# Unread products of constants on TensorE in five waits for norms, and low-part products chunk by chunk

## The chip, the core and the metric

The kernel runs on one core of a Trainium2 chip. Its time is the device time of one execution in microseconds (us); shown are the median of three executions and one execution taken with the hardware profiler. PE is TensorE, PEld its weight loads, DVE VectorE, ACT ScalarE, POOL GpSimd, SP the engine that issues the weight transfers. "L420" is line 420 of the kernel.

## What is computed

Two transformer stacks of two layers each, on 256 tokens of width 1024, all in float32. The parts that matter here are the norms and the projections behind them:

```python
def rms_norm(x, g):
    xf = x.astype(jnp.float32)
    y = xf * lax.rsqrt(jnp.mean(xf * xf, axis=-1, keepdims=True) + EPS)
    return y.astype(x.dtype) * g
...
# first_block, layer l (twice)
        x = x + gt1_x * (jnp.concatenate([oa, ob, oc], axis=-1) @ w_out[l])
        hx2 = modulate(rms_norm(x, g_norm2[l]), sh2_x, sc2_x)
        x = x + gt2_x * conv_ffn(hx2, w_up[l], conv_w[l], conv_b[l], w_down[l])
...
# second_block, layer l (twice)
        h = rms_norm_2(x, norm_mix_pre[l])
        proj = h @ w_in[l]
        ...
        x = x + rms_norm_2(merged @ w_out[l], norm_mix_post[l])
        h2 = rms_norm_2(x, norm_ffn_pre[l])
        gu = h2 @ w_ffn_in[l]
        f_g, f_u = jnp.split(gu, 2, axis=-1)
        f = (jax.nn.silu(f_g) * f_u) @ w_ffn_out[l]
        x = x + rms_norm_2(f, norm_ffn_post[l])
```

The first block also carries a second stream (`ctx`) of 256 tokens through its first layer.

## The kernel before

The activations stand transposed: eight chunks of 128 features by 256 tokens. A float32 operand is cut into a high part (type fp32r, written by ACT) and a low part (the rest, written by DVE or POOL), and a projection is three products of that type for each chunk: high by high, low weight by high, high weight by low. A weight tile is 1024 columns wide, which gives 128 output features in 24 products (L406, L407, L408 in `products`). SP brings the tiles in, ACT cuts off the high part (L1005) and DVE the low part (L1637); four cut tiles have room, and the room of a tile comes free when its last product is done (`lin`).

Each engine has its own program in a fixed order, written out as the Python code runs, and engines meet at semaphores. Results go to four PSUM banks in turn (`PS`); a fifth tile waits until the first one's bank has been read.

Where an activation has only just been normed, the first two weight tiles go through `two_tiles` instead. PE first takes the products with the high parts: for the first tile, chunk by chunk as ACT delivers (L420 and L421, each pair waits for `x_hi` of its chunk), then for the second tile, sixteen products with nothing to wait for. Then follow the products with the low parts (L428): all eight of the first tile, then all eight of the second. It is called 13 times. In the feed-forward of the second block `between` puts the eight sums of the `fpre` norm between the high and the low products.

A norm needs a sum over all 1024 features. ACT squares the chunks, PE adds them up by a product with a matrix of ones in plain float32 (`SquareSum`, L481), ACT takes the root (L1067), DVE the reciprocal (L1673), and then the normed chunks are made. A plain float32 product stands in the trace as two records, so the eight sums of a norm are 16 records. Three norms are summed in another form (`in_groups`): `x0`, `fpost` and `pre` of the second layer. There four squares are summed at a time, each on 32 columns of the array (L469), ACT copies the four partial sums out (L1064), and a product with the constant `four` adds them (L487) before ACT takes the root.

Five places are spoken of below, in order of time. At each, PE has finished the sums of a norm and waits for root, reciprocal and the first normed chunk:

- **A**: first block, second layer, before the feed-forward.
- **B**: between the first and the second block.
- **C**: second block, first layer, between `w_out` (norms `post` and `fpre`) and the feed-forward.
- **D**: second block, between its layers: norm `fpost`, then norm `pre`.
- **E**: as C, in the second layer.

Of the kernel before, what the change touches and what calls it, by code (L numbers as in the profile page):

```python
# [153 lines left out]
def build(nc, w_d, par_d, con_d, big_d, x_d, pos_d, out_d, widths):  # L154
    PAR, npar, CON, ncon = offsets()
    ctx = ExitStack()
    with ctx:
# [40 lines left out]
        ident, ones, eps = con("ident"), con("ones"), con("eps")  # L198
# [95 lines left out]
        def in_groups(tag):  # L294

            return tag == "x0" or tag[0] in ("fpost", "pre")
# [95 lines left out]
        def tensor(q):  # L392
# [18 lines left out]
            def two_tiles(src, at, between=None):  # L411
                us = [feed.next() for _ in range(2)]
                bk = [PS.take() for _ in us]
                for b, i in zip(bk, us):
                    w = weights(i, 8)
                    q.wait_ge(*cut(i))
                    wait(b.free)
                    for c in range(8):
                        q.wait_ge(*at[c][0])
                        e.matmul(b.ap[:, 0:256], w.hi[:, c], src[c].hi, start=c == 0, stop=False)  # L420
                        e.matmul(b.ap[:, 0:256], w.lo[:, c], src[c].hi, start=False, stop=False)  # L421
                if between is not None:
                    between()
                for b, i in zip(bk, us):
                    w = weights(i, 8)
                    for c in range(8):
                        q.wait_ge(*at[c][1])
                        last = e.matmul(b.ap[:, 0:256], w.hi[:, c], src[c].lo, start=False, stop=c == 7)  # L428
                    last.then_inc(*lin.mark(i))
                for i in us:  # L430
                    feed.release(i)
                return list(zip(bk, us))
# [11 lines left out]
            class SquareSum:  # L444
# [38 lines left out]
                def rstd(self, out):  # L483
# [4 lines left out]
                    self.bank.free = [roots(self.tag)]  # L488

# [174 lines left out]
            def feed_forward(tag, at, passed, early=None, between=None):  # L664
                bk, tiles = [], {}
                got = two_tiles(H8, at, between)
# [39 lines left out]
            for l in range(DEPTH):  # L706
# [87 lines left out]
                else:  # L794
                    ss_x.rstd(k.rst[0])
                    feed_forward(("ffn", l, 0), parts_of(("n2", l, 0)), convd)
# [5 lines left out]
                    ss.rstd(k.rst[0])  # L802

            for l in range(DEPTH):
                at = parts2_of(("pre", l))
                lows = []
                for n in range(2):
                    sq = SquareSum(("low", l, n), 2)
                    got = two_tiles(H8, at) if n == 0 else [tile(H8), tile(H8)]
# [169 lines left out]
                ss.rstd(k.rst[0])  # L979
                ss = SquareSum(("fpre", l), 8, k.sq2[0])  # L980
# [9 lines left out]
                if l + 1 < DEPTH:  # L990
                    ss = SquareSum(("pre", l + 1), 8)
# [4 lines left out]
                    ss.rstd(k.rst[0])  # L996

# [1908 lines left out]
```

## Time and profile before

| | us |
|---|---|
| median of three executions | 2258.08 |
| lowest, highest | 2256.72, 2259.97 |
| profiled execution, its own time | 2255.04 |
| span of its trace | 2253.2 |

The clock that the chip granted to PE is 0.972 of full speed in the mean: it is either full (2.4 GHz) or half (1.2 GHz). Busy time of PE is no measure of its work, since products overlap: a product of 256 columns lasts 0.28 us in the trace, but at full clock the next starts 0.117 us later. So the text counts from start to start. In a timeline row, the first number is the start and the second the length; "xN" says how many instructions are merged; the last bracket tells how long the engine was idle and which engine's instruction released it.

### The profile page before, as it was taken

To read this page: it belongs to the slowest core of one execution; us is meant where nothing else is said; L and a number is where in the kernel's file an instruction comes from. 1 tells how busy PE (TensorE), PEld (TensorE's weight loads), DVE (VectorE), ACT (ScalarE), POOL (GpSimd) and SP (SyncE) were. 2 spreads that over 40 slices of the span, in tenths; PEclk is the share of its full clock that TensorE was granted. 3 is DMA by queue.
4 is the path that set the end of the run, shared out by engine and by line. 5 is a ranking of instruction groups with operands and counts; after the bars stand their busy time and mean duration, and the time that the engine had idled before them with its cause. 6 is when DMAs were issued, how large, how long until landed. Compare 5 with 4: busy or idle time off the path is not lost.

```text
span 2253.2 us, 43766 instructions
## 1 busy us (share of the span) xinstructions
PE 2110.4 (94%) x18160; PEld 1970.9 (87%) x18160; DVE 1514.5 (67%) x2244; ACT 1150.2 (51%) x1919; POOL 561.5 (25%) x668
## 2 busy tenths in 40 slices
PE   6999989999999999899999989989997989999997
PEld 5986679999999886689988889989996889998997
DVE  3657766777777666668776769755556677865554
ACT  4535545555655643555556555554444655554443
POOL 0012321332333002213321144104330134212331
PEclk9999999999999998999999999999998999999999
DMA  8546544555555454345544335535552434453552
GB/s 345 178 143 230 206 169 147 191 188 171 168 196 184 140 163 159 129 143 192 191 159 155 131 118 183 179 121 197 188 188 105 158 114 150 144 196 133 190 191 85
DMA packets 103205, 378.37 MB, mean 168 GB/s; under 512 B 11456, under 2 KB 11744, under 8 KB 101984
## 3 DMA queue, kind: packets, MB, share of 16 engines
q1 hardware_dynamic: 101520, 367.31, 47.6%
q10 hardware_dynamic: 1488, 8.27, 1.0%
q8 instruction: 144, 2.36, 0.4%
q14 instruction: 53, 0.43, 0.1%
HBM read 374.49 MB, written 1.05 MB: 167 GB/s over the span
## 4 chain that ended last, share of the span: by engine, by line
PE 33%; issue 13%; POOL 5%; DVE 3%; ACT 3%; POOLq 0%; DVEq 0%; ACTq 0%
PE ps L406 10%; PE ps L408 10%; PE ps L407 10%; POOL R L2596 2%; POOL R L2638 1%; DVE WL L1637 1%; PE ps L481 1%; POOL R L2441 1%; PE ps L420 1%; POOL X L2399 1%; PE ps L421 1%; ACT WH L1005 1%; PE ps L428 1%; DVE RST L1673 1%; DVE TMP L1647 0%
## 5 line engine op out<-in xcount | busy, mean ns | idle before, releaser
L406 PE MATMUL ps<-X,WH 128*128 128x256 f32 x4384 | 1242.6, 283 | 15.3 <-DVE WL L1637 7.9
L407 PE MATMUL ps<-X,WH 128*128 128x256 f32 x4384 | 1228.4, 280 | 0.0
L408 PE MATMUL ps<-X,WL 128*128 128x256 f32 x4384 | 1227.4, 280 | 0.0
L1637 DVE TENSOR_TENSOR WL<-RAW,WH 128x1024 fp32r<-128x1024 f32 (+2 forms) x608 | 773.6, 1290 | 452.9 <-ACT WH L1005 451.1
L406 PEld LDWEIGHTS ps<-X,WH 128*128 128x128 f32 x4384 | 827.0, 189 | 30.0 <-DVE WL L1637 11.7
L407 PEld LDWEIGHTS ps<-X,WH 128*128 128x128 f32 x4384 | 826.9, 189 | 1.7
L408 PEld LDWEIGHTS ps<-X,WL 128*128 128x128 f32 x4384 | 826.9, 189 | 0.0
L1005 ACT ACTIVATE WH<-RAW 128x1024 fp32r<-128x1024 f32 (+2 forms) x608 | 623.8, 1045 | 263.6 <-PE ps L408 261.5
L2441 POOL TENSOR_SCALAR R<-CONS,SM 128x128 f32<-128x128 f32 x128 | 83.8, 666 | 319.6 <-DVE SM L1832 308.9
L2535 POOL TENSOR_TENSOR TMP<-TMP 128x256 f32<-128x256 f32 x66 | 48.9, 741 | 446.6 <-ACT TMP L1354 443.1
L1155 ACT ACTIVATE PB<-ps,SM 128x512 f32<-128x512 f32 (+1 forms) x152 | 87.6, 583 | 140.9 <-DVE SM L1822 140.5
L1647 DVE SCALAR_TENSOR_TENSOR TMP<-ps,PARS,TMP 128x255 f32<-128x255 f32 x264 | 124.2, 480 | 11.4 <-ACT TMP L1350 2.7
L1647 DVE SCALAR_TENSOR_TENSOR R<-R,PARS 128x256 f32<-128x256 f32 x180 | 109.7, 662 | 0.0
L2540 POOL TENSOR_TENSOR X<-TMP,X 128x256 fp32r<-128x256 f32 x66 | 103.6, 1570 | 5.3
L1350 ACT ACTIVATE TMP<-ps,PARS 128x256 f32<-128x256 f32 x132 | 71.5, 555 | 58.5 <-PE ps L408 52.1
L1822 DVE TENSOR_REDUCE SM<-ps 128x1 f32<-128x512 f32 (+2 forms) x136 | 77.1, 606 | 27.6 <-PE ps L609 26.9
L420 PE MATMUL ps<-X,WH 128*128 128x256 f32 x208 | 66.4, 344 | 30.5 <-ACT X L1609 10.6
L1354 ACT ACTIVATE TMP<-TMP 128x256 f32<-128x256 f32 x66 | 27.6, 418 | 116.1 <-DVE TMP L1647 116.1
L643 PEld LDWEIGHTS ps<-PTB,R 128*64 128x64 f32 x768 | 43.1, 139 | 49.5 <-issue 23.4
L2656 POOL TENSOR_TENSOR TMP<-TMP,RST 128x256 f32<-128x256 f32 x44 | 32.6, 741 | 210.4 <-ACT TMP L1617 210.3
L643 PE MATMUL ps<-PTB,R 128*64 128x128 f32 x768 | 59.6, 286 | 24.7 <-ACT PTB L1170 18.2
L420 PEld LDWEIGHTS ps<-X,WH 128*128 128x128 f32 x208 | 49.1, 236 | 36.9 <-issue 22.4
(194 smaller groups left out, 2204.0 us busy)
## 6 DMA issues: line engine op xcount, KB each, us to landing
RAW<-w_dram SPq DMA_DIRECT2D x674, 512.0 KB, 3.7
RAW<-w_dram SPq DMA_DIRECT2D x16, 480.0 KB, 3.2
BIG<-big_dram ACTq DMA_DIRECT2D x4, 1024.0 KB, 5.2
RAW<-w_dram SPq DMA_DIRECT2D x8, 320.0 KB, 2.7
RAW<-w_dram SPq DMA_DIRECT2D x6, 384.0 KB, 2.9
XT<-x_dram ACTq DMA_DIRECT2D x2, 1024.0 KB, 7.5
CONS<-con_dram ACTq DMA_DIRECT2D x1, 1169.0 KB, 9.7
out_dram<-XT SPq DMA_DIRECT2D x1, 1024.0 KB, 3.9
```

What stands on the lines that cost most here:

```text
L406: e.matmul(out, a.hi, b.hi, start=start and i == 0, stop=False, skip_group_check=open_bank)
L407: e.matmul(out, a.hi, b.lo, start=False, stop=False, skip_group_check=open_bank)
L408: last = e.matmul(out, a.lo, b.hi, start=False, stop=stop and i == n - 1, skip_group_check=open_bank)
L420: e.matmul(b.ap[:, 0:256], w.hi[:, c], src[c].hi, start=c == 0, stop=False)
L643: e.matmul(ob[0].ap[64 * s:64 * s + 64, c:c + 128], u["subs"][s]["v"][j], b[:, 128 * j:128 * j + 128], start=j == 0, stop=j == nk - 1)
L1005: e.activation(weights(i).hi, raw(i), ACT.Copy).then_inc(*w_hi.mark(i))
L1155: e.activation(ap, bank.ap[:, x * u["nk"]:x * u["nk"] + u["nk"]], ACT.Exp, bias=sm.ap[:, col:col + 1], accum_out=sm.ap[:, 4 + col:5 + col] ...
L1637: e.tensor_tensor(weights(i).lo, raw(i), weights(i).hi.bitcast(F32), ALU.subtract).then_inc(*w_lo.mark(i))
L1647: return e.scalar_tensor_tensor(out=out, in0=a, scalar=s, in1=b, op0=o0, op1=o1)
L1822: e.tensor_reduce(sm.ap[:, col:col + w], bank.ap[:, 0:w * nk].rearrange("p (x n) -> p x n", x=w), AX, ALU.max, negate=True).then_inc(*maxe ...
L2441: e.tensor_scalar(d.ap, ident, sm.ap[:, 8 + s:9 + s], None, ALU.mult).then_inc(*inverted.mark(tag, i, s))
L2540: e.tensor_tensor(a.ap.lo, bg.ap, a.ap.hi.bitcast(F32), ALU.subtract).then_inc(*gate_lo.mark(tag, j))
```

## The change

It adds a helper `keep_up(n, cols)` to the PE program. It issues n products of the matrix of ones with the constant `cosA`, in plain float32, into the next free PSUM bank. Nobody reads them, and no mark is set.

- `keep_up` stands behind the sums of a norm at A (6 products), B (6), C and E (11 each), and twice at D (9 behind `fpost`, 6 behind `pre`).
- In four of the 13 calls of `two_tiles` (`fill`: behind B, C, D and E) one product of 256 columns follows each chunk's high-part pair of the first tile (7 times), and one of 64 columns each chunk's low-part pair (7 times). At A the call has no such filling.
- In all 13 calls the low-part products go chunk by chunk: chunk 0 for both tiles, then chunk 1 for both, and so on.
- `fpost` and `pre` are no longer summed in groups; the form with eight products and no copy is used, for `fpost` of both layers and for `pre` of the second.

```diff
         def in_groups(tag):
-            return tag == "x0" or tag[0] in ("fpost", "pre")
+            return tag == "x0"
...
-            def two_tiles(src, at, between=None):
+            def two_tiles(src, at, between=None, fill=False):
...
                         e.matmul(b.ap[:, 0:256], w.lo[:, c], src[c].hi, start=False, stop=False)
+                        if fill and b is bk[0] and c < 7:
+                            keep_up(1)
                 if between is not None:
                     between()
-                for b, i in zip(bk, us):
-                    w = weights(i, 8)
-                    for c in range(8):
+                for c in range(8):
+                    for b, i in zip(bk, us):
                         q.wait_ge(*at[c][1])
-                        last = e.matmul(b.ap[:, 0:256], w.hi[:, c], src[c].lo, start=False, stop=c == 7)
-                    last.then_inc(*lin.mark(i))
+                        last = e.matmul(b.ap[:, 0:256], weights(i, 8).hi[:, c], src[c].lo, start=False, stop=c == 7)
+                        if c == 7:
+                            last.then_inc(*lin.mark(i))
+                    if fill and c < 7:
+                        keep_up(1, 64)
...
+            def keep_up(n, cols=256):
+
+                bank = PS.bufs[PS.n % len(PS.bufs)]
+                q.wait_ge(s_con2, 16)
+                wait(bank.free)
+                for _ in range(n):
+                    e.matmul(bank.ap[:, 0:cols], ones, con("cosA")[:, 0:cols], start=True, stop=True)
...
-                got = two_tiles(H8, at, between)
+                got = two_tiles(H8, at, between, fill=between is not None)
...
                     ss_x.rstd(k.rst[0])
+                    keep_up(6)
                     feed_forward(("ffn", l, 0), parts_of(("n2", l, 0)), convd)
...
                     ss.rstd(k.rst[0])
+                    keep_up(6)
...
-                    got = two_tiles(H8, at) if n == 0 else [tile(H8), tile(H8)]
+                    got = two_tiles(H8, at, fill=True) if n == 0 else [tile(H8), tile(H8)]
...
                 ss.rstd(k.rst[0])
+                keep_up(11)
                 ss = SquareSum(("fpre", l), 8, k.sq2[0])
...
                 if l + 1 < DEPTH:
+                    keep_up(9)
                     ss = SquareSum(("pre", l + 1), 8)
...
                     ss.rstd(k.rst[0])
+                    keep_up(6)
```

PE's program at D, before: the two grouped sums, then the first high-part pairs. `scaled`, `squares` and `parted` are marks of DVE and ACT, `ps` is PSUM, R and PB hold squares, CONS the constants.

```order
L469 MATMUL ps<-R,CONS 32x256 [waits scaled,squares]
L469 MATMUL ps<-R,CONS 32x256 x3
L469 MATMUL ps<-R,CONS 32x256 [waits squares]
L469 MATMUL ps<-R,CONS 32x256 x3
L487 MATMUL ps<-RST,CONS 128x256 [waits parted]
L469 MATMUL ps<-PB,CONS 32x256 [waits squares,scaled]
L469 MATMUL ps<-PB,CONS 32x256 x3
L469 MATMUL ps<-PB,CONS 32x256 [waits squares]
L469 MATMUL ps<-PB,CONS 32x256 x3
L487 MATMUL ps<-RST,CONS 128x256 [waits parted]
L420 MATMUL ps<-X,WH 128x256 [waits x_hi,w_lo]
L421 MATMUL ps<-X,WL 128x256
```

The same place of PE after the change, where L485 is the former L481 and L500 the product in `keep_up`:

```order
L485 MATMUL ps<-R,CONS 128x256 [waits squares]
L485 MATMUL ps<-R,CONS 128x256
L500 MATMUL ps<-CONS 128x256 x9
L485 MATMUL ps<-PB,CONS 128x256 [waits scaled,squares]
L485 MATMUL ps<-PB,CONS 128x256 [waits squares] x7
L500 MATMUL ps<-CONS 128x256 x6
L420 MATMUL ps<-X,WH 128x256 [waits x_hi,w_lo]
L421 MATMUL ps<-X,WL 128x256
L500 MATMUL ps<-CONS 128x256
L420 MATMUL ps<-X,WH 128x256 [waits x_hi]
L421 MATMUL ps<-X,WL 128x256
```

The product with `four` and its wait are gone, eight full products per norm stand in place of two groups of four, and every high-part pair has an unread product between it and the next.

PE's program at the end of the same call of `two_tiles` in B, before: the low-part products, the first tile's with their waits and then the second tile's.

```order
L428 MATMUL ps<-X,WH 128x256 [waits x_lo] x2
L428 MATMUL ps<-X,WH 128x256 [waits y_lo]
L428 MATMUL ps<-X,WH 128x256 [waits x_lo] x2
L428 MATMUL ps<-X,WH 128x256 [waits y_lo]
L428 MATMUL ps<-X,WH 128x256 [waits x_lo] x2
L428 MATMUL ps<-X,WH 128x256 x8
L406 MATMUL ps<-X,WH 128x256 [waits convd,w_lo]
```

And after (L429 is the former L428):

```order
L429 MATMUL ps<-X,WH 128x256 [waits x_lo]
L429 MATMUL ps<-X,WH 128x256
L500 MATMUL ps<-CONS 128x64
L429 MATMUL ps<-X,WH 128x256 [waits x_lo]
L429 MATMUL ps<-X,WH 128x256
L500 MATMUL ps<-CONS 128x64
```

The first tile's last product now stands next to last instead of eighth, and seven narrow products stand in between.

## Rows read from the trace of the kernel before

The columns of a window row are its start and end, its length, each engine's busy time with its instructions (x), PE's granted clock, the busy share of the DMA engines, and GB/s. A timeline row has start, length, engine, line and operation; the bracket holds the idle time before it and what ended it. Windows of one engine hold PE alone; windows of all engines hold PE, PEld, DVE, ACT and POOL.

**Rows 1.** The page: full products and their weight loads, busy and mean ns.

```profile
L406 PE MATMUL ps<-X,WH 128*128 128x256 f32 x4384 | 1242.6, 283 | 15.3 <-DVE WL L1637 7.9
...
L406 PEld LDWEIGHTS ps<-X,WH 128*128 128x128 f32 x4384 | 827.0, 189 | 30.0 <-DVE WL L1637 11.7
```

**Rows 2.** PE: feed-forward behind C by window; next long wait behind D.

```profile
1520.84:1700.04 179.20, 179.20 (x1538) 1.00 0.56 191
...
1754.53 0.36 PE L406 MATMUL ps<-X,WH 128*96 128x256 f32 x1 [1.80 <-ACT R L1424]
```

**Rows 3.** PE by windows at A to E, last sum to third tile.

```profile
977.31:989.14 11.83, 8.25 (x50) 0.71 0.15 51
1175.08:1187.05 11.97, 8.56 (x49) 0.71 0.05 17
1501.94:1520.84 18.90, 13.47 (x66) 0.73 0.07 26
1703.99:1726.79 22.80, 11.48 (x68) 0.63 0.03 9
2040.28:2059.65 19.37, 13.95 (x66) 0.74 0.06 23
```

**Rows 4.** Timeline of PE: first high-part product at C.

```profile
1507.02 0.55 PE L420 MATMUL ps<-X,WH 128*128 128x256 f32 x1 [4.91 <-ACT X L1609]
```

**Rows 5.** Timeline of PE in B: two products at half clock.

```profile
1183.75 0.41 PE L420 MATMUL ps<-X,WH 128*128 128x256 f32 x1
1183.96 0.41 PE L421 MATMUL ps<-X,WL 128*128 128x256 f32 x1
```

**Rows 6.** Timeline: eight float32 sums in C; weights of an 8-column product.

```profile
1515.52 3.62 PE L481 MATMUL ps<-R,CONS 128*128 128x256 f32 x16
...
192.41 0.30 PEld L497 LDWEIGHTS ps<-CONS,R 128*128 128x128 f32 x2 [1.21 <-DVE R L1702]
```

**Rows 7.** All engines by window, high-part products of an unfilled call.

```profile
1473.96:1479.48 5.52, 4.61 (x34) 3.99 (x33) 3.06 (x6) 4.51 (x9) 1.60 (x2) 1.00 0.35 123
```

**Rows 8.** All engines by window, the same pause in either layer.

```profile
1407.70:1414.70 7.00, 3.89 (x27) 3.54 (x26) 7.00 (x12) 0.84 (x2) 0.53 (x2) 1.00 0.24 74
1943.30:1950.30 7.00, 3.92 (x11) 3.05 (x10) 7.00 (x12) 0.84 (x2) 0.52 (x2) 0.66 0.24 78
```

**Rows 9.** Timeline of ACT: eight high parts at A, five at B.

```profile
980.41 3.30 ACT L1087 ACTIVATE X<-TMP,SM 128x256 fp32r<-128x256 f32 x8 [2.42 <-DVE TMP L1647]
...
1178.09 2.00 ACT L1392 ACTIVATE X<-TMP 128x256 fp32r<-128x256 f32 x5 [2.34 <-DVE TMP L1647]
```

**Rows 10.** Timeline of ACT: the last two high parts in C.

```profile
1510.62 0.90 ACT L1609 ACTIVATE X<-XT,PARS 128x256 fp32r<-128x256 f32 x2
```

**Rows 11.** Timeline of PE: first grouped sum of D, whole sum at B.

```profile
1701.61 1.19 PE L469 MATMUL ps<-R,CONS 128*32 128x256 f32 x16 [1.42 <-ACT R L1053]
...
1171.55 3.69 PE L481 MATMUL ps<-R,CONS 128*128 128x256 f32 x16 [1.33 <-DVE XT L1647]
```

**Rows 12.** Timeline of ACT at D: root, last squares, second root.

```profile
1704.09 0.47 ACT L1067 ACTIVATE RST<-ps,CONS 128x256 f32<-128x256 f32 x1 [0.79 <-PE ps L487]
...
1711.63 0.72 ACT L1044 ACTIVATE PB<-XT 128x256 f32<-128x256 f32 x2 [0.18 <-PE ps L469]
...
1715.38 0.47 ACT L1067 ACTIVATE RST<-ps,CONS 128x256 f32<-128x256 f32 x1 [1.31 <-PE ps L487]
```

**Rows 13.** Timeline, last norm: PE's first sums, ACT's root.

```profile
2238.94 0.64 PE L469 MATMUL ps<-R,CONS 128*32 128x256 f32 x8
...
2241.71 0.47 ACT L1067 ACTIVATE RST<-ps,CONS 128x256 f32<-128x256 f32 x1 [0.79 <-PE ps L487]
```

**Rows 14.** Timeline in `w_out`: ACT's first square, PE's first sum.

```profile
1480.62 0.38 ACT L1044 ACTIVATE PB<-ps 128x256 f32<-128x256 f32 x1 [0.92 <-PE ps L428]
...
1481.35 0.60 PE L481 MATMUL ps<-PB,CONS 128*128 128x256 f32 x2
```

**Rows 15.** Timeline of PE: sums behind the first call of `two_tiles`.

```profile
43.94 3.72 PE L481 MATMUL ps<-R,CONS 128*128 128x256 f32 x16 [1.26 <-ACT R L1053]
```

## The prediction

> **What bounds the kernel now.** I read the page first, then PE by windows, then the timelines at the places that the diff touches. The table ahead has the span, 2253.2 us; the execution's own time is 2255.04, and the median, 2258.08, lies 3.0 above. Over long stretches PE is the bound: behind C it runs 64 weight tiles, 1536 products, in 179.2 us without a pause at full clock [rows 2]. That is 0.117 us from start to start and 2.8 a tile, though each lasts 0.283 [rows 1], and whatever delays PE there delays the end. The pauses stand where a norm must be known. At the five places of the change PE waits between the last sum and the first high-part product, 4.9 us at C [rows 4] and about 3.5 at A and B, and the granted clock in the windows from the last sum to the third weight tile is 0.63 to 0.74 of full [rows 3]: it falls to half in the pause and comes back in or behind the products. At half clock they start 0.21 us apart [rows 5]. The chain in the pause (root, reciprocal, scaling) is ACT's and DVE's and doesn't care for PE's clock. So what a full clock can give back is only in the products behind it, and it must be weighed against what the unread products cost once real work is ready.
>
> **Prices.** Eight float32 sums are 16 records in 3.62 us [rows 6], of which the last one's length beyond its step is some 0.17 (0.283 less 0.117, as for a real product): 0.215 a record, 0.43 a product of 256 columns at full clock. A filled pair then takes 2 x 0.117 + 0.43 = 0.665 us, an unfilled one 0.235. For 64 columns no row exists. By columns alone it would be a quarter, 0.11 us. But each of its two records also loads 128 columns of weights, and the two loads of an 8-column product take 0.30 us together, 0.11 more than the 0.189 of one [rows 1, 6]; in the stream of real products a record never costs under 0.117 [rows 2]. I take 2 x 0.117 = 0.23, nearest to that row, and keep 0.11 and, above, 0.43 for the range. Seven of them cost 1.6 us a call.
>
> The Trainium skill (FP8 and Floating Point Precision, TensorE Precision Notes) says that true FP32 takes four passes through the array. For 64 columns this would be 4 x 64 / 2.4 GHz = 0.11 us, and the 28 narrow products would cost 3.5 us less than in my sum. TensorE: Matmul & The Clock Gate, LDWEIGHTS (loading the stationary operand), has a weight load depend on its columns alone, 128 / 1.2 = 107 ns each, whatever the product's width; the row's 0.11 agrees with it.
>
> **Does the clock hold?** At A, B, D the six unread products cover 2.6 of some 3.5 us, at C and E eleven cover 4.7 of 4.9. The rest, about 1 us, is far below any pause behind which the clock fell here: the same 3.4 us pause was followed by full clock in one layer and by 0.66 in the other [rows 8]. Nor do paused high-part pairs bring it down: an unfilled call took 5.52 us at 1.00 [rows 7]. I take full clock at all five.
>
> **A** (no filling). Eight high parts come 0.4 us apart, the last at 983.71 [rows 9]. The last pair of the first tile then ends near 984.1, 16 products of the second tile at 985.98, 16 low-part ones at 987.85. The low parts follow the high ones 2.6 us behind, and going by chunks lets PE start on them without a wait. Before: 989.14 [rows 3]. **-1.3.**
>
> **B** (filled). The high parts come 0.4 apart [rows 9], but a filled pair takes 0.665: now PE, not ACT, sets the pace. From 1178.6, plus 0.1 for a start out of idleness, 7 x 0.665 + 0.235 gives 1183.55; 16 products, 1185.4; 16 low-part products and seven narrow ones, 1.87 + 1.6, 1188.9. Before: 1187.05. **+1.9.**
>
> **C and E** (filled). The high parts come slower here, the last at 1511.52 [rows 10], so the filling costs only 0.3: first tile done at 1512.1, second 1513.95, eight sums 1517.4, low parts 1520.9. Before: 1520.84, and that with half clock in much of it. **0.** E paid 19.37 for what C did in 18.90 [rows 3]; in the profiled execution it would gain 0.4. That is chance, so I count E as C.
>
> **D.** The first grouped sum starts at 1701.61 [rows 11] and its root at 1704.09 [rows 12]. A whole sum needs 3.7 us from its start to the root [rows 11], 1705.3: +1.2, on the chain. For `pre` the four last squares end at 1712.35 and the root follows only at 1715.38, 3.0 later: four products, a copy and the product with `four`, at half clock [rows 12]. Eight products keep up with the squares, and only one is left behind the last: 0.9. That gives 2.1 back, net -0.9. The filling is B's: from 1717.8 to 1728.1. Before: 1726.79. **+1.3.**
>
> **Last norm.** Sums start at 2238.94, root at 2241.71 [rows 13]. Whole: 16 x 0.215 + 0.2 = 3.65 from the start, 2242.6. Nothing stands behind it but the chain to the output. **+0.9.**
>
> **Low parts by chunks, elsewhere.** The first tile ends seven products (0.8 us) later, the second at the same time. This costs where somebody waits for the first one. Behind `w_out`, PE's first sum waits for ACT's square of it: 1480.62 to 1481.00, the sum at 1481.35 without a wait [rows 14]. Now the square starts at 1481.4, the sum at 1481.9: +0.65, twice. **+1.3.** In the first call the sums wait for ACT too [rows 15], behind its square and copy of both tiles, which now come together: **+0.4.** In the other calls ACT's work on the first tile has slack, since bank and weights are due 5.6 us later: 0. PE waited for no low part, so the new order gains nothing. DMAs and SP's queue are untouched.
>
> **Sum:** -1.3 + 1.9 + 0 + 0 + 1.3 + 0.9 + 1.3 + 0.4 = +4.5 us (4.1 against the profiled execution, with E's 0.4). The terms before rounding (-1.29, 1.86, 0.05, 0, 1.35, 0.88, 1.30, 0.45) give 4.6. On the median: 2258.1 + 4.6 = 2262.7.
>
> **Rivals.**
> (1) *The delay behind B and D is taken up.* PE's next long wait behind D, 1.8 us, ends with ACT's L1424 [rows 2]. If ACT's and DVE's chain before it doesn't start from PE's third tile, B's and D's 1.9 + 1.3 vanish: 2259.5. Against it: that chain starts with PE's sums of `low`, which stand behind those tiles.
> (2) *Narrow products cost their columns only*, 0.11: 28 x 0.12 = 3.4 less, 2259.3.
> (3) *Faster.* The profiled execution was 3.0 below the median. If that is half clock that others pay at these five places, it is gone now, and the sum starts from 2255.0: 2259.2; with (2) as well, 2255.8, and with (1) too, 2252.6. It decides from all three together on. For it: the length of a half-clock stretch is chance [rows 3, 8]. Against it: the rest of the kernel has such stretches too.
> (4) *The clock falls all the same.* Then filling is dear: at half clock a filled pair takes 1.3 us. Seven more expensive pairs and 16 products at 0.21, +6 us at B and at D each: up to 2274.
>
> The Trainium skill (TensorE: Matmul & The Clock Gate, Why this matters for your kernels) asks for no idle gap over some 3 us, which speaks against the filling: the 1 us left by the six products would be harmless by it. No run here shows B without filling; by the working of A it would end 3 us earlier.
>
> **How the numbers follow.** The measurement tells a change of about 0.2%, 4.5 us, from none: slower begins at 2262.6, faster below 2253.6. Forecast as worked out, give or take 2 us: 0.60, of which 0.40 above 2262.6, since the half-clock stretches of other executions can be shorter than those profiled. (1) 0.10 and (2) 0.10, both no change. (3) 0.10, of which 0.06 faster. (4) and a narrow product at 0.43 (5.6 more): 0.10, slower. Together: slower 0.40 + 0.10 = 0.50, faster 0.06, within 0.2% the other 0.44. The likeliest case is spread over the edge; its own range is 2260 to 2265.5. The range from (2) with part of (3) to the dear end: 2256.5 to 2268.5.
>
> **What would show it.** A profile of the changed kernel should have: a clock of 1.00 at A to E; starts 0.215 apart in the unread products of 256 columns and 0.117 in those of 64; at B and D no idleness between high-part pairs, and 10.3 us from the first of them to the third tile; at A 6.9; sums of the last norm in 3.7 us; PE's first sum behind `w_out` 0.6 us later than the low parts' end. The prediction is wrong if the narrow records start closer, if the wait behind D shrinks by what the tiles lost, or if the clock is below 1 in any of the five.

## The result, and the profile after

The changed kernel is slower by 0.41%: median 2266.72 us of eight executions (2261.11 to 2270.97) against 2256.43 of before (2252.84 to 2260.34), ratio 1.0041, 95% interval 1.0029 to 1.0053, or 9.2 us (6.5 to 12.0); the two medians as they stand are 10.3 us apart. A second set of executions of both kernels gave 1.0035 (1.0023 to 1.0048). The forecast was 2262.7, 4.6 us more than before. The direction held, and 2266.7 lies in the range of 2256.5 to 2268.5, but above the likeliest case of 2260 to 2265.5; the forecast change was about half of the measured one.

The profiled execution took 2261.11 us, the shortest of the eight, with a span of 2259.3 us and a mean clock of 0.984 (before: 2253.2 us and 0.972). So the clock rose as the change meant it to, and the kernel still lost time. The lines are moved: L429 is the former L428, L485 the former L481, L500 the unread product; L1061, L1070, L1084, L1409, L1441 and L1654 are the former L1044, L1053, L1067, L1392, L1424 and L1637.

PE by windows in the changed kernel, from the last sum to the third tile, places A to E (the answers to [rows 3]; columns as there):

```profile
980.44:990.97 10.53, 9.54 (x61) 1.00 0.12 44
1177.43:1191.30 13.87, 13.05 (x90) 1.00 0.09 30
1504.67:1523.67 19.00, 18.83 (x115) 1.00 0.07 25
1707.98:1730.98 23.00, 21.19 (x124) 1.00 0.05 18
2045.97:2064.96 18.99, 18.83 (x116) 1.00 0.07 25
```

The clock is 1.00 in all five, where it was 0.63 to 0.74. A is 1.3 us shorter. B is 1.9 longer although its clock rose from 0.71. C is 0.1 longer and E 0.4 shorter. D by this window is 0.2 longer, but it begins behind `fpost`'s sums; with these it is 1.35 longer, as shown below.

Timeline of PE at B: the filled pairs, and the narrow products between low-part products.

```profile
1181.20 0.28 PE L421 MATMUL ps<-X,WL 128*128 128x256 f32 x1
1181.32 0.59 PE L500 MATMUL ps<-CONS 128*128 128x256 f32 x2
...
1181.87 0.28 PE L421 MATMUL ps<-X,WL 128*128 128x256 f32 x1
...
1188.10 0.33 PE L500 MATMUL ps<-CONS 128*128 128x64 f32 x2
1188.24 0.48 PE L429 MATMUL ps<-X,WH 128*128 128x256 f32 x2
1188.56 0.33 PE L500 MATMUL ps<-CONS 128*128 128x64 f32 x2
```

Read the starts. From one filled pair to the next (1181.20 to 1181.87) it is 0.67 us, forecast 0.665. From one pair of low-part products with its narrow product to the next (1188.10 to 1188.56) it is 0.46, of which the pair is 0.23: the narrow product costs 0.23, as taken. One sign did not come as forecast: the two records of a narrow product start 0.055 us apart, not 0.117. Its price holds all the same, since the real products beside it are held up for the rest.

Timeline of PE at D, from `fpost`'s first sum to the first high-part product:

```profile
1704.45 3.69 PE L485 MATMUL ps<-R,CONS 128*128 128x256 f32 x16 [1.42 <-ACT R L1070]
1707.98 4.05 PE L500 MATMUL ps<-CONS 128*128 128x256 f32 x18
1712.88 4.40 PE L485 MATMUL ps<-PB,CONS 128*128 128x256 f32 x16 [0.85 <-ACT PB L1061]
1717.11 2.75 PE L500 MATMUL ps<-CONS 128*128 128x256 f32 x12
1720.68 0.36 PE L420 MATMUL ps<-X,WH 128*128 128x256 f32 x1 [0.82 <-ACT X L1409]
```

and of ACT there, the two roots and the last squares between them:

```profile
1708.18 0.47 ACT L1084 ACTIVATE RST<-ps,CONS 128x256 f32<-128x256 f32 x1 [3.32 <-PE ps L485]
...
1714.81 1.34 ACT L1061 ACTIVATE PB<-XT 128x256 f32<-128x256 f32 x4 [0.48 <-DVE XT L2349]
1717.31 0.47 ACT L1084 ACTIVATE RST<-ps,CONS 128x256 f32<-128x256 f32 x1 [1.16 <-PE ps L485]
```

The root of `fpost` comes 3.73 us behind the first sum (2.48 in [rows 11, 12]), that of `pre` 1.16 behind the last square (3.03). First sum to third tile is 1730.98 - 1704.45 = 26.53; before it was 1726.79 - 1701.61 = 25.18. PE's next long wait behind D is still there at its length, 27.75 us behind the third tile (27.74 before [rows 2]), so this delay isn't taken up there:

```profile
1758.73 0.36 PE L406 MATMUL ps<-X,WH 128*96 128x256 f32 x1 [1.81 <-ACT R L1441]
```

Timeline in `w_out` (answers to [rows 14]) and in the last norm (to [rows 13]):

```profile
1483.54 0.38 ACT L1061 ACTIVATE PB<-ps 128x256 f32<-128x256 f32 x1 [1.74 <-PE ps L429]
1483.98 0.70 PE L485 MATMUL ps<-PB,CONS 128*128 128x256 f32 x2 [0.36 <-ACT PB L1061]
...
2244.16 3.61 PE L485 MATMUL ps<-R,CONS 128*128 128x256 f32 x16
2247.81 0.47 ACT L1084 ACTIVATE RST<-ps,CONS 128x256 f32<-128x256 f32 x1 [2.86 <-PE ps L485]
```

PE's first sum now waits 0.36 us for ACT's square where it did not wait, and the call with its sum takes 8.26 us instead of 7.63. The last norm's root comes 3.65 us behind the first sum, where it came 2.77 behind.

So every term of the sum that stood for something is there at its size, and yet the median moved by twice the sum. The spans of the two profiled executions differ by 6.1 us, of which the terms are 4.1 (with E's 0.4, as the forecast had it for this pair). Stretches between the places that were to stay the same differ by 2.8 us one way and 2.1 the other, with 2.0 left over. Where the rest comes from is the question of the experiments.

### The profile page after: what moved, and what is told of

Read it like the earlier page. It is cut to its first block, busy times and chain, and to the rows that moved or that the text cites. A ratio compares the mean times of both kernels' runs of the same rounds, so it can differ in the third digit from the quotient of the medians.

```text
span 2259.3 us, 44160 instructions
## 1 busy us (share of the span) xinstructions
PE 2138.5 (95%) x18364; PEld 1998.7 (88%) x18364; DVE 1514.9 (67%) x2244; ACT 1148.6 (51%) x1916; POOL 561.3 (25%) x668
## 4 chain that ended last, share of the span: by engine, by line
PE 33%; issue 13%; POOL 5%; DVE 4%; ACT 2%; POOLq 0%; DVEq 0%; ACTq 0%
PE ps L406 10%; PE ps L407 9%; PE ps L408 9%; POOL R L2613 2%; POOL R L2655 1%; DVE WL L1654 1%; PE ps L485 1%; POOL R L2458 1%; PE ps L500 1%; POOL X L2416 1%; ACT WH L1022 1%; PE ps L420 1%; PE ps L429 1%; DVE RST L1690 1%; DVE TMP L1664 1%
## 5 line engine op out<-in xcount | busy, mean ns | idle before, releaser
L406 PE MATMUL ps<-X,WH 128*128 128x256 f32 x4384 | 1242.0, 283 | 17.8 <-DVE WL L1654 8.8
L407 PE MATMUL ps<-X,WH 128*128 128x256 f32 x4384 | 1226.7, 280 | 0.0
L1654 DVE TENSOR_TENSOR WL<-RAW,WH 128x1024 fp32r<-128x1024 f32 (+2 forms) x608 | 773.7, 1290 | 459.2 <-ACT WH L1022 457.5
L406 PEld LDWEIGHTS ps<-X,WH 128*128 128x128 f32 x4384 | 825.4, 188 | 31.4 <-DVE WL L1654 12.7
L407 PEld LDWEIGHTS ps<-X,WH 128*128 128x128 f32 x4384 | 825.6, 188 | 1.6
L1664 DVE SCALAR_TENSOR_TENSOR TMP<-ps,PARS,TMP 128x255 f32<-128x255 f32 x264 | 124.1, 480 | 11.8 <-ACT TMP L1367 3.1
L2557 POOL TENSOR_TENSOR X<-TMP,X 128x256 fp32r<-128x256 f32 x66 | 103.5, 1569 | 5.3
L2655 POOL TENSOR_TENSOR R<-R,TMP 128x256 f32<-128x256 f32 x48 | 38.7, 821 | 154.4 <-DVE TMP L2295 154.4
L2681 POOL TENSOR_TENSOR X<-TMP,X 128x256 fp32r<-128x256 f32 x44 | 73.9, 1680 | 3.5
```

The source lines that it names most:

```text
L406: e.matmul(out, a.hi, b.hi, start=start and i == 0, stop=False, skip_group_check=open_bank)
L407: e.matmul(out, a.hi, b.lo, start=False, stop=False, skip_group_check=open_bank)
L1654: e.tensor_tensor(weights(i).lo, raw(i), weights(i).hi.bitcast(F32), ALU.subtract).then_inc(*w_lo.mark(i))
L1664: return e.scalar_tensor_tensor(out=out, in0=a, scalar=s, in1=b, op0=o0, op1=o1)
L2557: e.tensor_tensor(a.ap.lo, bg.ap, a.ap.hi.bitcast(F32), ALU.subtract).then_inc(*gate_lo.mark(tag, j))
L2681: e.tensor_tensor(a.ap.lo, b.ap, a.ap.hi.bitcast(F32), ALU.subtract).then_inc(*gate_lo.mark(("glu", l), j))
```

## The experiments

Twelve runs were made: nine new kernels, and before, the changed kernel and one of the nine a second time. Ratios are to the executions of before in the same set, with 95% intervals; 0.001 is 2.3 us. "Call" is the time from the first high-part product of `two_tiles` to the third tile.

### How much of it is before's own spread

> The kernel before, unchanged, to see how much its executions differ and with what clock. The changed kernel lost 9.2 us in the medians (6.5 to 12.0), but the terms of the forecast, which its profile bears out place by place, give 4.6. Theory: the profiled execution of before (2255.0 us, clock 0.972) paid more at the five places than its executions do on average, since the clock falls and comes back at other moments; then the executions here spread over some 8 us, with clocks from 0.970 to 0.980, and in a second profile the five windows from the last sum to the third tile together are shorter than the 84.9 us of the first by 1 to 5 us. Rival: the five windows are as long as in the first profile within 1 us, and the difference arises in stretches that the change doesn't touch.

> The changed kernel, unchanged, for a second set of executions. Its profile bore out every term of the forecast within 0.1 us, which sum to 4.6 us, but its median lay 9.2 us (6.5 to 12.0) above before. Executions of before alone spread from 2249 to 2261 us. Theory: the surplus is chance of that spread in 8 executions; here the median is 2261 to 2265, ratio to before 1.003 (1.0015 to 1.004). Rival: the surplus is real and lies in stretches that the change doesn't touch: 2266 to 2268, ratio 1.004 or above, and the stretches from the first narrow call of two_tiles to the next two (266.46 and 185.10 us in the first profile, 263.69 and 182.60 in that of before) are again 2 us longer each.

Measured: before against itself 1.0002 (0.999 to 1.0015). Twelve executions took 2252.91 to 2261.55 us, with clocks of 0.969 to 0.977. In its profile the five windows are together 0.7 us shorter than in the first, so the rival held. That what separates executions of before, some 9 us, lies elsewhere is likely but not shown, since only a few executions have a profile. Four profiles with before's form at the five places (these two and two from below) gave calls of 7.9 to 8.2 us at A, 8.2 to 8.5 at B, 13.5 to 14.4 at C and E. The half clock there was not dearer in the profiled execution than it commonly is.

The changed kernel again: 1.0035 (1.0023 to 1.0048), median 2263.31, as the theory had it. The calls at A to E are the same to 0.02 us as in its first profile. Of the stretches named in the rival, the one up to the narrow call (the third call of `two_tiles`, at some 370 us) had 264.9 us, so that surplus doesn't come every time; the one behind it had 183.7 where before had 182.6 in both profiles. That one goes with the order, as the next three kernels show.

### The filling, and the order of the low parts

`no_fill`, then `order_back` on top of it, then `order_alone`, which is before with the new order and nothing else:

```diff
-                got = two_tiles(H8, at, between, fill=between is not None)
+                got = two_tiles(H8, at, between, fill=False)
...
-                    got = two_tiles(H8, at, fill=True) if n == 0 else [tile(H8), tile(H8)]
+                    got = two_tiles(H8, at) if n == 0 else [tile(H8), tile(H8)]
```

```diff
-                for c in range(8):
-                    for b, i in zip(bk, us):
+                for b, i in zip(bk, us):
+                    w = weights(i, 8)
+                    for c in range(8):
...
```

> The changed kernel without the unread products inside two_tiles (28 of 256 and 28 of 64 columns gone); those in the waits stay, and the order of low parts and the whole sums too. Theory: the clock is held by the products in the waits alone, so B and D take A's 6.8 us from first high-part product to third tile where they took 10.3, -3.5 each; C and E lose 7 x 0.23 for the narrow ones and 0.3 for the wide ones, -1.9 each. Together -10.8 us against the changed kernel's 2266.7: 2255.9, ratio to before 0.9998 (0.9985 to 1.001). Rival: without the filling the clock falls in the pauses between the pairs, as it did before; B, D stay at 8.0 to 8.4 us, C and E at 13.8 to 14.3, and the kernel takes some 2262, ratio 1.0025.

> As no_fill, and the low parts tile by tile again, as before the change. Theory: going by chunks costs 0.65 us behind each w_out and 0.45 in the first call, and nothing elsewhere, so this is 1.75 us below no_fill; ratio to before 0.999 (0.9978 to 1.0002). In the profile PE's first sum in w_out stands 7.6 us behind the first high-part product again, not 8.26. Rival: with the clock full at A to E the first tile's low parts now come too late (2.6 us behind the high ones), PE waits for them at A, B, D, and what is won at w_out is lost there: same time as no_fill.

> The kernel before with nothing but the low parts chunk by chunk in all 13 calls. Theory: +0.65 behind either w_out and +0.4 in the first call, nothing elsewhere: ratio 1.0008 (0.9995 to 1.002); in the profile the calls behind w_out take 8.26 us where they took 7.63. Rival: the difference of 3.8 us between the two kernels without filling, with and without this order (2258.07 and 2254.29), is the order's own, so that there is another cost, of the first tile of the other calls coming 0.8 us later: ratio 1.0017 or above, with another stretch that is longer by 1 us or more in the profile.

Measured: `no_fill` 0.9998 (0.9988 to 1.0009), `order_back` 0.9989 (0.9976 to 1.0002), `order_alone` 1.0007 (0.9995 to 1.0019).

`no_fill` has the ratio that the theory gave, but its theory, that the waits' products alone hold the clock, is only half true. PE by windows in the calls at B to E, and behind the fall at D:

```profile
1182.95:1190.19 7.24, 6.86 (x48) 1.00 0.02 3
1511.86:1525.49 13.63, 12.11 (x64) 0.87 0.00 0
1722.51:1731.03 8.52, 8.15 (x48) 0.80 0.13 40
2052.76:2065.86 13.10, 11.70 (x65) 0.87 0.01 1
...
1725.03:1728.44 3.41, 3.41 (x17) 0.50 0.00 0
```

B takes 7.24 us instead of 10.29. The filling does have an effect: without it, with the waits still filled, C, D and E fell to half clock for 3.4 us here, at a price of 1.0 to 1.6 us each. At D PE had been idle for 0.82 us ahead of the call and 0.37 in it, no longer at a time. In the four profiles of this form (these waits filled, no filling in the calls) half clock came never at A and B, twice in four at D, and five times in eight at C and E. Against a call at full clock the filling costs 3.1 us at B and at D, and 1.8 at C and at E with its narrow products. Against the mean of the four profiles, half clock included (7.24, 7.87 and 13.0), it costs 3.1 at B, 2.4 at D and 0.9 at C and at E: 7.3 us for which nothing comes back.

`no_fill` and `order_back` differ by 3.8 us in the medians and by 2.0 in the ratios, where 1.75 was expected, and the ratio of `order_alone`, 1.6 us (-1.1 to 4.3), is that of its theory, while its interval just takes in the rival's 1.0017. The times don't decide it. The profile of `order_alone` shows two further delays. First, behind the call at A. ACT in before, then in `order_alone` (third tile at 989.14 and at 995.08):

```profile
989.34 0.56 ACT L1350 ACTIVATE TMP<-ps,PARS 128x256 f32<-128x256 f32 x1 [0.37 <-PE ps L428]
989.92 1.28 ACT L1354 ACT_TABLE_LOAD   x1
...
991.54 2.94 ACT L1005 ACTIVATE WH<-RAW 128x1024 fp32r<-128x1024 f32 x3
```

```profile
995.16 1.02 ACT L1350 ACTIVATE TMP<-ps,PARS 128x256 f32<-128x256 f32 x2 [4.59 <-PE ps L427]
996.20 1.28 ACT L1354 ACT_TABLE_LOAD   x1
...
998.02 2.94 ACT L1005 ACTIVATE WH<-RAW 128x1024 fp32r<-128x1024 f32 x3
```

Both evictions now come at once, so the table load stands 1.12 us behind the third tile's start where it stood 0.78 behind, and the weight splits behind it in ACT's program, L1005, and then DVE's are 0.54 late (998.02 is 2.94 behind the third tile, 991.54 is 2.40). Nobody waits for them at once. PE runs into it 26 us later, in `order_alone`:

```profile
1020.85 0.38 PE L406 MATMUL ps<-X,WH 128*128 128x256 f32 x1 [0.39 <-DVE WL L1637]
```

This wait, some 26 us behind the third tile, stands in all six profiles with the new order and in none of the eight with the old one. From the third tile at A to the first high-part product at B it is 189.5 us in all eight and 190.0 to 190.1 in all six: +0.54.

Second, behind the narrow call at 370 us. PE's next wait there ends with the root of a norm. Timeline of PE in before and in `order_alone`, and the windows of 6 us behind the wait:

```profile
404.40 0.38 PE L406 MATMUL ps<-X,WH 128*128 128x256 f32 x1 [1.70 <-ACT RST L1067]
```

```profile
411.09 0.38 PE L406 MATMUL ps<-X,WH 128*128 128x256 f32 x1 [1.97 <-ACT RST L1067]
```

```profile
404.40:410.40 6.00, 5.50 (x44) 1.00 0.30 104
```

```profile
411.09:417.09 6.00, 6.00 (x38) 0.72 0.36 111
```

The pause is 0.27 us longer and ends 0.54 later behind the call's third tile (31.54 us, before 31.00), and behind it the clock falls. In all six profiles with the new order there is half clock of 3.4 us here and in none of the eight with the old one. The time from the narrow call to the next call of `two_tiles` is 182.6 us in six of these eight (184.0 in the other two) and 183.7 in four of the six (185.1 in the other two): +1.1, of which 0.54 is there when the pause ends and the other 0.6 comes behind it, with the half clock. That the longer pause brought the clock down fits all fourteen profiles, but no run changed the pause alone.

### The sums alone, and in groups again

`sums_alone` against before, and `fpost_grouped` against `order_back`:

```diff
-            return tag == "x0" or tag[0] in ("fpost", "pre")
+            return tag == "x0"
```

```diff
-            return tag == "x0"
+            return tag == "x0" or tag[0] == "fpost"
```

> The kernel before with nothing but whole sums for fpost and pre. Theory: the last norm's root comes 0.9 us later; at D fpost's root 1.2 later. The eight products for pre, which at full clock leave only 0.9 us behind the last square, fall behind the squares here: the clock is half at D, a whole product takes 0.86 us, the squares come in pairs 1.2 us apart, so the root for pre stands 8 x 0.86 = 6.9 us behind the first square at 1708.73 plus what fpost's delay adds: 1716.8, where it was 1715.38. Together +1.4 and +0.9: ratio 1.001 (1.000 to 1.0025). Rival: pre's whole sums give back 2.1 us at half clock too, so D loses nothing net: -0.9 + 0.9 = 0, ratio 1.0000, and the root for pre comes before 1715.5 relative to the same start.

> As order_back, and fpost of both layers summed in groups again; pre of the second layer stays whole. Theory: the last norm's root comes 0.9 us earlier and that of fpost at D 1.2 us earlier, both on the chain, -2.1 against order_back: some 2252.1 by the medians so far, ratio to before 0.998 (0.9968 to 0.9995), faster than both kernels. Rival: at D the gain is lost, since pre's first squares come from DVE, which is busy with the tiles of fpost either way; then -0.9 only.

> fpost_grouped once more, in other executions. Its six executions lay 7.9 us below before, 0.9963. By places and profiles the sum is: A -1.3, B -1.1, C and E -0.9 each, D -0.7 in the call and -1.65 ahead of it (root of fpost no later, pre whole), 0 elsewhere: -6.5 us, 0.9971. Theory: ratio 0.9971 (0.996 to 0.9985), in the profile the calls at A, B, D at 6.8, 7.2 and 7.2 us. Rival: the six were lucky with half clock elsewhere, and by the forecast's own terms (-2.1 against order_back at 0.9989) it is 0.998.

Measured: `sums_alone` 1.0007 (0.9998 to 1.0016), `fpost_grouped` 0.9963 (0.9949 to 0.9977) and again 0.9958 (0.9942 to 0.9973).

ACT at D in `sums_alone`, where PE's first sum starts at 1705.45:

```profile
1709.18 0.47 ACT L1067 ACTIVATE RST<-ps,CONS 128x256 f32<-128x256 f32 x1 [3.33 <-PE ps L481]
...
1719.32 0.47 ACT L1067 ACTIVATE RST<-ps,CONS 128x256 f32<-128x256 f32 x1 [2.17 <-PE ps L481]
```

First sum to the root of `pre` takes 13.87 us; in before it takes 1715.38 - 1701.61 = 13.77. So the theory, that whole sums fall behind the squares at half clock, falls, by the profile: the clock is back before they are through (16 records in 5.41 us against 4.40 at full clock), and `pre` gives back what `fpost` loses. Only the last norm costs: from the third tile at E to the end it takes 194.3 us instead of 193.5. The ratio lies between theory (1.001) and rival (1.0000) and excludes neither.

`fpost_grouped` is faster than both kernels: by 0.37 and 0.42% against before and some 0.8% against the changed one. It keeps the unread products in the waits and whole sums for `pre`, and drops the filling, the new order and `fpost`'s whole sums. Calls at C, D and E in the second profile, PE by windows:

```profile
1503.19:1515.28 12.09, 10.57 (x65) 1.00 0.00 0
1711.04:1719.51 8.47, 8.09 (x48) 0.80 0.12 43
2040.01:2053.65 13.64, 12.12 (x65) 0.87 0.01 1
```

The places give -6.5 us, as its expectation has it; the ratios say -8.3 and -9.5. Both times it came out below the expected range (0.9968 and 0.996). The first expectation put it 2.1 us below `order_back`; it lay 4.9 below in the medians. Two to three us of its gain have no place in the profiles; in the second one D's call even took 8.5 us where 7.2 was expected. How much of the gain is the waits' products and how much `pre`'s whole sums was not run apart.

### Price and purpose of the unread products

`double_fill` and `fill_no_waits` (here B's line; the others likewise) against the changed kernel:

```diff
                         if fill and b is bk[0] and c < 7:
-                            keep_up(1)
+                            keep_up(2)
```

```diff
                     ss.rstd(k.rst[0])
-                    keep_up(6)
+                    keep_up(0)
```

`half_waits` (`keep_up(3)` for 6, 5 for 11, 4 for 9) and `ce_fill` against `fpost_grouped`:

```diff
                     ss.rstd(k.rst[0])
-                    keep_up(6)
+                    keep_up(3)
```

```diff
-                got = two_tiles(H8, at, between, fill=False)
+                got = two_tiles(H8, at, between, fill=tag[0] == "glu")
```

> The changed kernel with two unread products of 256 columns instead of one behind each of the seven high-part pairs (28 more in all). Theory: each costs its two records of 0.215, 0.43 us, on the path: B and D go from 10.29 to 13.3 us, C and E, where a pair has 0.04 of slack, from 13.92 to 16.7. Together +11.6 us against the changed kernel, ratio to before 1.0085 (1.0065 to 1.010). Rival: the stationary operand is the same for both, so the second costs only half, 0.215, as columns alone would have it: +5.6, ratio 1.006 or less, and records half as far apart.

> The changed kernel with the filling in two_tiles, but without the unread products in the waits. Theory (rival 4 of the forecast): the clock falls in the waits as it did before, so the filling is issued at half clock, where a filled pair takes some 1.3 us. A goes back to 8.0 us from first high-part product to third tile, B and D go from 10.3 to some 13.2, C and E from 13.9 to some 17.5: together +14.3 us against the changed kernel, ratio to before 1.010 (1.008 to 1.013). Rival: since PE is busy between the pairs, the clock comes back sooner behind the pause than before (half clock of some 3.4 us in each call instead of 4.6 to 9.4); then B and D take 11.8 and C, E 15.4: ratio 1.007.

> The fastest kernel so far (fpost_grouped: unread products in the waits alone, low parts tile by tile, fpost in groups) with about half of the unread products: 3, 3, 5, 4, 3, 5 instead of 6, 6, 11, 9, 6, 11. Theory: what counts is how long PE stays idle. About 2.4 us are left empty at A, B, D and 3 at C and E, and a pause of 2.2 us behind the narrow call was followed by half clock in five profiles of five, one of 2.0 us in none of five. So in two or more of the five calls of the profile there is half clock again, of up to 5 us, and the kernel is 2 to 5 us slower than fpost_grouped. Rival: any work in the pause is enough; then A and B take 6.78 and 7.24 us, D 7.24, and the time is that of fpost_grouped within 1.5 us.

> fpost_grouped with the seven unread products of 256 columns back in the calls of C and E alone (no narrow ones there: keep_up(1, 64) comes with the filling, so they are back as well, 7 x 0.23). Theory: at C and E the filling holds the clock, but with its narrow products costs as much as it gives: 13.92 us against a mean of 13.0 (12.08 or 13.1 to 13.6, as the clock holds or not) in the six calls without it. So +0.9 each: 1.8 us slower than fpost_grouped. Rival: the pauses between the pairs there are what brings the clock down behind them too (the sums' stretch and the products after it), so that the stretches behind C and E get shorter than 198 us by more than 1 and the kernel is faster than fpost_grouped.

**double_fill**: 1.0082 (1.0068 to 1.0095), 11.9 us behind the changed kernel of the same set, expected 11.6. PE's timeline:

```profile
1184.50 1.03 PE L500 MATMUL ps<-CONS 128*128 128x256 f32 x4
...
1185.61 1.02 PE L500 MATMUL ps<-CONS 128*128 128x256 f32 x4
```

A pair with two takes 1.11 us (1184.50 to 1185.61), 0.44 more than with one: the price is that of two records each, the same stationary operand or not. The calls took 13.32 at B and D, 16.78 at C and E.

**fill_no_waits**: 1.0064 (1.0042 to 1.0086), of four executions. Near the rival's 1.007; the interval leaves out the theory's 1.010. PE in the calls at A to D (E took 15.34 us at 0.89):

```profile
986.85:994.91 8.06, 8.06 (x48) 0.68 0.07 17
1184.97:1195.26 10.29, 10.29 (x76) 1.00 0.13 41
1517.23:1532.86 15.63, 15.63 (x93) 0.87 0.00 1
1730.88:1741.18 10.30, 10.30 (x77) 1.00 0.10 38
```

A is back at 8.06. C and E have 3.9 and 3.3 us of half clock, about as the rival said; for B and D it had said 11.8 us, and they took 10.3. But at B and D the clock was never low in the call, nor at B in the empty pause before it, though that is as long as before. The pause and call at B in before, then the same pause in `fill_no_waits`:

```profile
1175.08:1178.65 3.57, 0.16 (x2) 0.84 0.00 0
1178.65:1187.05 8.40, 8.40 (x48) 0.66 0.07 25
```

```profile
1181.39:1184.97 3.58, 0.17 (x1) 1.00 0.00 0
```

This is one profile. It does show that 3.6 us with nearly nothing on PE need not bring the clock down. The trace of before has both outcomes for one and the same shorter wait: 1.8 us, 27.7 us behind the third tile, at B and at D. The 4 us behind it:

```profile
1214.78:1218.78 4.00, 3.62 (x17) 0.57 0.01 2
...
1754.53:1758.53 4.00, 2.59 (x20) 1.00 0.00 0
```

**half_waits**: 1.0003 (0.9986 to 1.0021), 9.3 us above `fpost_grouped` of the same set. PE in the calls at A to D:

```profile
978.82:986.52 7.70, 7.70 (x49) 0.78 0.04 9
1176.02:1184.30 8.28, 7.90 (x48) 0.79 0.06 16
1506.92:1521.04 14.12, 12.91 (x64) 0.76 0.00 1
1717.26:1724.66 7.40, 7.40 (x48) 0.77 0.01 4
```

Half clock in these and, with 14.24 us at 0.76, at E, so in all five, behind pauses of which 2.1 to 2.8 us were empty. The rival fell, and the theory held for the clock, not for the size, which it put at 2 to 5 us: half the products buy nothing that can be measured. The five calls account for 3.5 to 4.8 us of the 9.3; the rest has no place in the profile, whose execution was one of the short ones (2252.3 us, median 2256.6).

The Trainium skill (TensorE: Matmul & The Clock Gate, Why this matters for your kernels) asks for no idle gap over some 3 us. The traces differ both ways: idle stretches of 1.9 to 2.8 us were followed by half clock eleven times (six behind the narrow call, five here), and that of 3.4 us in the 3.58 us window above was not.

**ce_fill**: 0.9971 (0.9958 to 0.9985). The kernel that ran has the wide products only; with the low parts tile by tile there is no place for the narrow ones, so the bracket in the expectation and its +0.9 a call don't apply to it. Both calls took 12.35 us at a clock of 1.00, where unfilled ones with filled waits took 12.1 three times and 13.1 to 13.6 five times (mean 13.0). So 0.6 us each is won in the profile. The medians (2250.73 against 2247.28) say rather the opposite, with overlapping intervals: not settled.

## Why the prediction was right or wrong

| step of the forecast | forecast | first two profiles, changed against before |
|---|---|---|
| clock at A to E | 1.00 | 1.00 |
| A, first pair to third tile | 6.9, term -1.3 | 6.78, -1.3 |
| B | 10.3, term +1.9 | 10.29, +1.9 |
| C, E | 13.9, term 0 | 13.92, +0.1 and -0.4 |
| D | term +1.3 | +1.35 |
| last norm | +0.9 | +0.88 |
| each `w_out` | +0.65 | +0.63 and +0.66 |
| first call | +0.4 | +0.47 |
| low parts by chunks in the other calls | 0 | behind the narrow call +2.5 here, +1.1 over all fourteen profiles; behind A +0.54 |

**Right: prices and paces.** An unread product of 256 columns costs 0.43 us, the narrow one 0.23, and with real work ready PE pays the wide one in full (`double_fill`) and the narrow one too (the 0.46 us step at B). Neither number needed a trace of the new code: the first came from the sums, the second from the step of the real products, 0.117 us a record. That the narrow records themselves would start 0.117 apart was wrong (0.055). Rival (2), columns alone, is out. So is rival (1), as far as the next waits go: that of 1.8 us, 27.7 us behind the third tile, follows B and D at the same distance and length in both profiles. Further on, untouched stretches differ by more than these delays. Rival (4) was right that filling can be issued at half clock (C in `fill_no_waits`), but the waits' products keep it from that.

**Right, for a reason that doesn't hold: the clock.** It was full at A to E in both profiles of the changed kernel. The forecast's reason was that the 1 us left of each wait is far below any pause behind which the clock fell. Yet in the trace of before it is 0.50 from 177.40 to 180.80 with no idle stretch over 0.6 us in the 7 us ahead, and in `no_fill` it fell at D behind 0.82 and 0.37. Where the waits were filled and the calls were not, the calls at C, D and E had half clock in 7 of 12 cases; in the changed kernel, with both filled, in none of 6.

**Wrong: the slack that was given to the other calls.** The step was: "ACT's work on the first tile has slack, since bank and weights are due 5.6 us later: 0." It looked at the consumer of that tile. What was late was what stands behind it on ACT: a table load and three weight splits, and DVE's halves behind these. They delayed PE 26 us on, by 0.54. In the other place a pause grew by 0.27, and half clock came with it, 1.1 in all. By these places the order costs 1.75 + 1.6 = 3.3 us; the times allow it (1.6 for `order_alone`, up to 4.3) and don't prove it. Corrected, the sum is 6.2 us.

**Open.** 6.2 lies within the second measurement (5.2 to 10.8) and just below the first (6.5 to 12.0). Some 2 to 3 us have no proven place. One candidate: half clock that begins between 255 and 259 us, ahead of the narrow call, stood in four of six profiles with the new order and in none of eight with the old, and makes the stretch up to the narrow call some 2 us longer. It is one of many places where a difference could have shown by chance, no wait grew there, and no run was made for it.

**Right for a partly lucky reason.** C and E were set at 0 from two numbers that happen to meet, 3.5 us of filling and its delays against the half clock. The forecast also started from the median of three executions, 2258.1; that of the eight is 2256.4. So the time is only 4.0 us off, while the change is off by 4.6 or more. The range held because its upper end took in a narrow product at 0.43 us, which is not what happened; with the missed 1.6 the forecast would have been 2264.3.

## What to carry to other kernels

Fill a wait with work that nobody reads only up to the moment at which real work may start, and fill it nearly whole: half of it bought nothing, and the same products between real ones cost their full price on the bound engine (3.1 us a call at B, where no half clock came without them, and 3.1 at D to avoid 1.3 in two profiles of four). When two results that came apart now come together, follow the program of the engine that consumes them, not only the consumer's own due time; the delay surfaced 26 us later at another engine. Trial each part of a bundled change alone: here the products in the waits, with `pre`'s whole sums, were worth some 8 to 9 us, and the other parts of the change ate that and about as much again.

## What the runs showed of the hardware

- Records of an unread product of 64 columns start 0.055 us apart, yet the real products around them are held up, so that the product costs 0.23 us. The distance of its own records would have said half of that, 0.11.
- A pause of 2.22 to 2.25 us, start to start, was followed by half clock six times in six; one of 1.95 to 1.99 at the same place was not, eight times in eight. Some 0.6 us went with it. This holds for that place alone: elsewhere the clock fell behind 1.8 us, or with no idle stretch over 0.82 (`no_fill` at D), and stayed behind 3.4 (`fill_no_waits` at B). The length of a pause by itself doesn't say what the clock will do.
- Executions of one kernel on one core spread over 9 to 12 us (2249.03 to 2260.97 in 29 executions of before), with mean clocks from 0.970 to 0.977. In profiles of the same code, untouched stretches differ by the half-clock pieces in them (the stretch up to the narrow call took 263.6 to 265.0 us with the old order, the one from D to the second `w_out` 283.3 to 288.5). Two profiles alone can't tell a difference below some 5 us; the times of single calls in them can, to 0.05 us.
